# The norms behind two attentions in two parts, in a two-block transformer kernel on one Trainium2 core

## The reference

```python
# block 1: two attentions side by side, 8 heads of 64 each
oa = dsa_attention(...)          # (1, 512, 512)
ob = forgetting_attention(...)   # (1, 512, 512)
o = jnp.concatenate([rms_norm(oa, g_out_a), rms_norm(ob, g_out_b)], axis=-1)
x = x + gate_m * (o @ w_out)     # 1024 x 1024
h = rms_norm(x, g_ffn) * (1.0 + scale_f) + shift_f
g_logits = h @ w_group ...; e_all = h @ w_router ...        # 4 + 32 columns, then the experts

# block 2: differential attention, 8 heads of 128, 768 keys
o = diff_attention(q, k_all, v_all, lam)                    # (1, 512, 8, 128)
o = rmsnorm(o, subln_g) * (1.0 - lam_init)                  # per head
y_attn = o.reshape(B, L, ATTN_OUT) @ w_branch_attn          # 1024 x 1024
y = (g_attn * y_attn + g_sgu * y_sgu) @ w_out
```

## Time and profile before

| | µs |
|---|---|
| median of 3 runs | 2796.1 |
| lowest and highest | 2791.27, 2798.64 |
| the profiled execution, its own time | 2799.37 |
| its span | 2797.6 |
| PE busy in it | 2667.5 (95%) |
| mean granted PE clock, share of full | 0.973 |

### The profile page before, as it was taken

How to read it: one execution, slowest core, us unless ns; L and a number is a source line. 1 busy time by engine, 2 the same in 40 slices (tenths; PEclk the granted TensorE clock), 3 DMA queues, 4 the chain that set the end, 5 groups by cost and what they waited for, 6 DMA issues and landing times. The chain is left out here.

```text
span 2797.6 us, 37221 instructions
## 1 busy us (share of the span) xinstructions
PE 2667.5 (95%) x14205; PEld 2184.3 (78%) x14209; DVE 1795.8 (64%) x3171; ACT 1074.9 (38%) x1724; POOL 922.6 (33%) x468
## 2 busy tenths in 40 slices
PE   8998898889999999999899999999999999999999
PEld 5776784333477878878787899999999978888887
DVE  7959442111142537439754099998998967889888
ACT  3225733223243322137633233334555533333333
POOL 0011122222224430112141357886322224455542
PEclk9996999999999999999999999999999999999999
DMA  8830048999633345300322147886689799999995
GB/s 354 310 114 1 3 160 332 386 400 381 256 131 121 122 173 196 126 25 1 121 90 93 61 140 249 300 297 218 238 306 327 286 354 387 376 397 393 388 407 219
DMA packets 135471, 646.34 MB, mean 231 GB/s; under 512 B 21536, under 2 KB 22432, under 8 KB 91040
## 3 DMA queue, kind: packets, MB, share of 16 engines
q1 hardware_dynamic: 86224, 485.11, 46.1%
q0 software_dynamic: 48384, 158.38, 15.1%
q10 hardware_dynamic: 720, 0.96, 0.1%
HBM read 620.25 MB, written 75.50 MB: 249 GB/s over the span
## 5 line engine op out<-in xcount | busy, mean ns | idle before, releaser
L195 PE MATMUL psum<-h_hi,w_hi 128*128 128x384 f32 (+1 forms) x1808 | 664.0, 367 | 18.3 <-DVE h_lo L575 4.4
L197 PE MATMUL psum<-h_hi,w_lo 128*128 128x384 f32 (+1 forms) x1808 | 651.8, 361 | 0.0
L196 PE MATMUL psum<-h_lo,w_hi 128*128 128x384 f32 (+1 forms) x1808 | 651.8, 360 | 0.0
L176 POOL TENSOR_TENSOR w_lo<-ring,w_hi 128x2048 fp32r<-128x2048 f32 x45 | 210.5, 4678 | 730.0 <-ACT w_hi L169 547.5
L195 PEld LDWEIGHTS psum<-h_hi,w_hi 128*128 128x128 f32 x1808 | 341.9, 189 | 54.4 <-issue 24.0
L196 PEld LDWEIGHTS psum<-h_lo,w_hi 128*128 128x128 f32 x1808 | 341.9, 189 | 32.6 <-issue 1.9
L197 PEld LDWEIGHTS psum<-h_hi,w_lo 128*128 128x128 f32 x1808 | 341.2, 189 | 33.0
L2589 ACT ACTIVATE w_hi<-ring 128x2048 fp32r<-128x2048 f32 x127 | 242.5, 1909 | 215.8 <-PE psum L197 196.6
L195 PE MATMUL psum<-w_hi,a_hi 128*128 128x512 f32 x768 | 300.8, 392 | 5.6 <-DVE w_lo L2597 5.6
L196 PE MATMUL psum<-w_lo,a_hi 128*128 128x512 f32 x768 | 299.7, 390 | 0.0
L197 PE MATMUL psum<-w_hi,a_lo 128*128 128x512 f32 x768 | 299.6, 390 | 0.0
(11 more groups left out here) (494 smaller groups left out, 4637.7 us busy)
## 6 DMA issues: line engine op xcount, KB each, us to landing
ring<-in_weights SPq DMA_DIRECT2D x199, 1024.0 KB, 6.9
w_expert_in<-in_experts_in SPq DMA_DIRECT2D x32, 2048.0 KB, 12.2
hid_dram<-hid_acts SPq DMA_DIRECT2D x64, 384.0 KB, 5.2
gates_dram<-block_gates SPq DMA_DIRECT2D x24, 1024.0 KB, 11.3
hid_tiles<-hid_dram SPq DMA_DIRECT2D x62, 384.0 KB, 7.7
gate_tiles<-gates_dram SPq DMA_DIRECT2D x15, 1536.0 KB, 13.0
o<-in_ada_later SPq DMA_DIRECT2D x16, 1024.0 KB, 6.3
w_expert_down<-in_experts_down SPq DMA_DIRECT2D x16, 1024.0 KB, 12.0
```

Source lines behind the costliest of these rows:

```text
L176: eng.tensor_tensor(lo, slot(k, n), hi.bitcast(F32), ALU.subtract).then_inc(k.w_ready, 1)
L195: k.nc.tensor.matmul(out, hi, x_hi, start=start, stop=False)
L196: k.nc.tensor.matmul(out, hi, x_lo, start=False, stop=False)
L197: return k.nc.tensor.matmul(out, lo, x_hi, start=False, stop=stop)
```

## The change

Each norm is cut into an early part and a late part. The early part holds the groups of columns that the attention finishes first: columns 512 to 1023 at the first joint (4 chunks), heads 0 to 6 at the second (7 chunks). Its sums, root, inverse, scaling and turns now stand in the attention stage, ahead of the barrier: DVE and ACT do their share between the last units, PE turns behind its last weighing (`turn_early`). The late part stays in the second stage. The contraction order of `first_products` puts the early chunks first (`norm.order`), and PE turns the late pieces at step 2 (first joint) or step 5 (second). Before the first product PE gets 8 idle products (`keep_going`). ACT splits the next weight tile (`between`) ahead of the late chunks instead of behind all eight. The `before` load loses its wait (it now goes to columns 512 to 639 of row tile 3). The scratch for sums, gains and the idle cell lies in tiles that exist already.

```diff
-def first_products(k, pe, outs, tile, source, done, ready):
+def first_products(k, pe, outs, tile, source, done, norm, turn_late_at):
     wait_split(k, pe, tile)
     hi, lo = parts(k, tile)
-    for kc in range(KC):
-        ready(min(kc + 1, KC - 1))
+    for step, kc in enumerate(norm.order):
+        if step == turn_late_at:
+            norm.turn_late(pe)
+        norm.split(pe, max(step, 1))
...
 class HeadNorm:
...
+        self.early, self.late = early, range(early.stop, self.groups) if early.start == 0 else range(0, early.start)
+        self.order = [g * per_group + c for part in (self.early, self.late) for g in part for c in range(per_group)]
...
     def vector(self, dve):
...
+        self.sum_squares(self.late)
+        low(0)
+        low(1)
+        self.invert(dve, self.late, 1)
+        for t in self.by_vector(self.late_by_scalar):
+            self.scale_by_vector(t, self.late)
+        for step in range(2, KC):
+            low(step)
...
+    def scalar(self, act, between):
...
+        high(0)
+        high(1)
+        self.root(act, self.late, 1)
...
+        for t in self.late_by_scalar:
+            self.scale_by_scalar(t, self.late)
+        for step in range(2, self.n_early):
+            high(step)
+        between()
+        for step in range(self.n_early, KC):
+            high(step)
...
@@ attention_stage: early = group 1, ACT scales row tile 3 early and tiles 2, 3 late
+                norm.turn_early(pe)
...
+                    if t == n:
+                        dve.wait_ge(square_done, 2 * first_sparse)
+                        norm.sum_early(dve)
+                    if t == n + 1:
+                        norm.invert_early(dve)
+                        for i in norm.by_vector(norm.early_by_scalar):
+                            norm.scale_by_vector(i, norm.early)
...
+                    if t == n:
+                        norm.load_root()
+                        norm.root_early(act)
+                    if t == n + 1:
+                        square(t - DEEP - 3)
+                    if t == n + 3:
+                        norm.scale_early_by_scalar(act)
...
@@ out_projection_stage
-                norm.rows_read(sp)
                 sp.dma_start(before, k.d["before"]).then_inc(consts, 16)
...
-                norm.tensor(pe)
-                first_products(k, pe, [k.psum[:, c] for c in range(2)], first, (k.h_hi, k.h_lo), done, lambda kc: norm.split(pe, kc))
+                keep_going(k, 7, 8)
+                first_products(k, pe, [k.psum[:, c] for c in range(2)], first, (k.h_hi, k.h_lo), done, norm, 2)
...
@@ diff_attention_stage: early = heads 0 to 6, ACT scales row tile 3 early and none late
+                pe.wait_ge(out_copied, n - 1)
+                norm.turn_early(pe)
...
+                    if t == n + 1:
+                        dve.wait_ge(square_done, n - TT)
+                        norm.sum_early(dve)
+                        norm.invert_early(dve)
+                    if t > n:
+                        norm.scale_by_vector(t - n - 1, norm.early)
...
+                    if t == n + 3:
+                        norm.scale_early_by_scalar(act)
                     if t > DEEP + 1:
                         square(t - DEEP - 2)
+                    if t == n:
+                        norm.load_root()
+                        norm.root_early(act)
```

More of the change, by code:

```diff
@@ L659, in attention_stage @@
     DEEP = 3
+    norm = k.norm = HeadNorm(k, k.squares[:], k.head_total, k.vecs[:, G_OUT:G_OUT + KC], range(1, 2), ((3,), (2, 3)))
     def new_keys(q):
@@ new lines, in __init__, with part, rows, sum_squares @@
+        self.gains, self.idle = k.head_gains, k.head_idle
+    def part(self, view, groups):
+        return view[:, :, groups.start:groups.stop]
+    def rows(self, t, groups):
+        return self.k.o[:, t, groups.start * self.width:groups.stop * self.width].rearrange("p (g n) -> p g n", g=len(groups))
+    def sum_squares(self, groups):
+        nc, total = self.k.nc, self.part(self.total, groups)
+        if self.squares.shape[-1] > 1:
+            self.k.vstep(nc.vector.tensor_reduce(total, self.part(self.squares, groups), AX.X, ALU.add))
+        nc.vector.tensor_scalar(total, total, 1.0 / self.width, EPS, ALU.mult, ALU.add).then_inc(self.k.head_norm_sems[0], 1)
@@ new lines, in scale_by_scalar, with by_vector, sum_early @@
+    def scale_by_scalar(self, t, groups):
+        for g in groups:
+            part = self.k.o[:, t, g * self.width:(g + 1) * self.width]
+            ins = self.k.nc.scalar.activation(part, part, ACT.Copy, scale=self.total[:, t, g:g + 1])
+        ins.then_inc(self.k.head_norm_sems[2][self.turn], 1)
+    def by_vector(self, by_scalar):
+        return [t for t in range(TT) if t not in by_scalar]
+    def sum_early(self, dve):
+        self.sum_squares(self.early)
+        self.k.vstep(self.k.nc.vector.tensor_scalar(self.gains, self.gain, self.gain_scale, None, ALU.mult))
@@ new lines, in invert_early, with load_root, root, root_early @@
+    def invert_early(self, dve):
+        self.invert(dve, self.early, 0)
+    def load_root(self):
+        self.k.nc.scalar.activation(self.idle, self.k.eps[:, 0:1], ACT.Sqrt)
+    def root(self, act, groups, half):
+        std_ready, rooted = self.k.head_norm_sems[0], self.k.head_norm_sems[5]
+        total = self.part(self.total, groups)
+        act.wait_ge(std_ready, 4 * self.turn + 2 * half + 1)
+        self.k.nc.scalar.activation(total, total, ACT.Sqrt).then_inc(rooted, 1)
+    def root_early(self, act):
+        self.root(act, self.early, 0)
@@ new lines, in scale_early_by_scalar, with turn_rows @@
+    def scale_early_by_scalar(self, act):
+        act.wait_ge(self.k.head_norm_sems[0], 4 * self.turn + 2)
+        for t in self.early_by_scalar:
+            self.scale_by_scalar(t, self.early)
+    def turn_rows(self, pe, chunks, by_scalar, scaled_earlier):
+        k, nc = self.k, self.k.nc
+        _std_ready, scaled, scaled_by_scalar, turned, _copied, _rooted = k.head_norm_sems
+        by_vector = self.by_vector(by_scalar)
+        order = (*by_vector, *by_scalar)
+        for t in order:
+            if t in by_vector:
+                pe.wait_ge(scaled[self.turn], scaled_earlier[0] + by_vector.index(t) + 1)
+            else:
+                pe.wait_ge(scaled_by_scalar[self.turn], scaled_earlier[1] + by_scalar.index(t) + 1)
+            for c in chunks:
+                mm = nc.tensor.transpose(k.psum[:, self.order.index(c), t * P:(t + 1) * P], k.o[:, t, c * P:(c + 1) * P], k.ident[:])
+                if t == order[-1]:
+                    mm.then_inc(turned, 1)
@@ new lines, in scalar, with high @@
+    def scalar(self, act, between):
+        k, nc = self.k, self.k.nc
+        def high(step):
+            c = self.order[step]
+            act.wait_ge(k.head_norm_sems[3], KC * self.turn + step + 1)
+            nc.scalar.activation(self.parts[0][:, c], k.psum[:, step], ACT.Copy, scale=self.gains[:, c:c + 1]).then_inc(k.activation_high, 1)
+        high(0)
+        high(1)
+        self.root(act, self.late, 1)
+        if self.late_by_scalar:
+            act.wait_ge(k.head_norm_sems[0], 4 * self.turn + 4)
+        for t in self.late_by_scalar:
[5 more added lines that the diff above has]
+            high(step)
@@ L1050, in rows_read, with split @@
+    def split(self, pe, step):
+        pe.wait_ge(self.k.head_norm_sems[4], KC * self.turn + step + 1)
     def rows_read(self, eng):
@@ L2423, in stat @@
                 mm.then_inc(stat_done, 1)
[L2425 to L2426 removed]
+            keep_going(k, 7, 8)
+            first_products(k, pe, [k.psum[:, c] for c in range(2)], first, (branch_hi, branch_lo), branch_done.sem, norm, 5)
             for c in range(2, KC):
```

113 lines of the change are left out of this document (44 added, 69 removed).

## The result

| | median µs (lowest, highest) | ratio to the kernel before, 95% interval |
|---|---|---|
| before, measured beside it | 2798.59 (2790.61, 2805.11) | |
| the changed kernel | 2804.02 (2797.05, 2810.77) | 1.0022 (1.0014, 1.0030) |
| its profiled execution | 2805.09, span 2803.3 | |

One of the 20 executions of the changed kernel, a slow one of 10543.77 µs, is left out of its highest time and of the ratio. 1.0022 of 2797 is +6.2 µs, with an interval of +3.9 to +8.4 (the two medians of the table differ by 5.4); the forecast was +2.6. The whole interval lies above no change and within 0.3%. The page answers the earlier trace rows: PE's busy time grew by 9.6 µs and its count by 32 rows. These are the idle products, 8 at each joint; each makes two rows in the trace (x16), and the 8 take 2.02 µs in a wait. The other 5.6 µs of busy time are the same work; the mean granted clock fell from 0.973 to 0.971.

A forecast was written before the change was run, and what follows sets the result against it. PE, busy 95% of the span, was taken as the bound, with late loads holding both joints: first +0.3 + 0.9 = +1.2, second -0.4 + 1.8 = +1.4, sum +2.6 µs, giving 2798.7 against the median 2796.1; range 2791 to 2804.

The forecast's parts named there:

- Both norms leave the path, the barriers come 1.0 and 2.5 µs later.: Both joints: early norm work moves into the attention stage; the barriers come 1.0 µs later at the first, 2.5 at the second.
- The small load comes out behind the 6 MB wherever it is issued, and the first joint stays bound by it.: First joint: `before` lands behind the same 6 MB at 369.9, so PE's bias products start +0.3 µs later.
- x becomes the last of the three at the second joint.: Second joint: x lands at 1393.4, behind gates and u, and releases DVE's first gating step; -0.4 µs.
- The clock at the second joint, 1.8.: Second joint: PE's granted clock falls behind its 4.5 µs pause, costing 2.2 or 1.5 µs; 1.8 taken.
- The clock at the first joint, 0.9.: First joint: bias products and first logits run at a lowered clock behind PE's wait; bounds 0 and 2.2 µs, 0.9 taken.
- PE is the bound behind it and nothing gives the time back.: Behind the second joint: PE bounds the kernel, so that joint's loss of +1.4 µs is not recovered.
- the first (the clock costs nothing net): Both joints: loads bound, slow clock stretches replace the old ones one for one; +0.3 - 0.4, 2796.0 µs; chance 0.20.
- The second and third: First joint: small load lands early, 2791.8 µs, chance 0.08; both joints: PE's side decides, 2785.5 µs, chance 0.05.
- The fourth: Both joints: turns ahead of the barriers take 0.22 instead of 0.11 µs each; +5.9, 2802.0 µs; chance 0.15.
- The signs that the prediction listed: Both joints: `before` within 0.5 µs of w_expert_down, PE waits 5 to 6 and some 4, x releases gating, barriers later.

The follow-up runs named there:

- the second joint alone: Change made at the second joint only, the first joint's code as in the kernel before: median 2799.51 µs, ratio 1.0009 to the kernel before.
- the load edits: Changed kernel with the small load `before` issued first and x on its own semaphore: median 2784.74 µs, ratio 0.9958 to the kernel before.

## Why the prediction was wrong

Step by step, as it stood:

- **Both norms leave the path, the barriers come 1.0 and 2.5 µs later.** Right: 351.05 against 347.80 and 1377.89 against 1373.19, net 0.8 and 2.4, or 1.1 and 2.7 with the delay of the reference copies. The turns ran at 0.12 µs each.
- **The small load comes out behind the 6 MB wherever it is issued, and the first joint stays bound by it.** Right in mechanism, shown by moving it to the front: 17.1 µs became 1.7, and the share at the logits went from +3.2 to -7.4. The size was near: +0.3 forecast; +0.9 in the trace after, +0.1 to +0.4 in the five others with this joint and load, 0.3 more in each from the copies ahead.
- **x becomes the last of the three at the second joint.** Right, shown by waiting for it apart, and by the same edit doing nothing in the old kernel. -0.4 forecast, +0.6 measured (+0.2 to +0.6 over the traces), 0.3 more from the copies ahead: the barrier's share was right, but x took 18.0 µs instead of the 16.9 that I carried over from the earlier trace rows. This step failed by about 1 µs.
- **The clock at the second joint, 1.8.** Measured 1.9 at chunk 4 (1.9 to 2.1 in five traces, 2.8 in the one with the second joint alone).
- **The clock at the first joint, 0.9.** This term failed most within the joints. It was 2.3 up to the logits, 2.5 to 2.7 in the five other traces, above the upper bound of 2.2 that the text gave. I took less than half of the bound because the products behind the wait are small and "only partly array time". The trace says that they are wholly so: 16 of them took 3.60 µs at half clock and 1.87 at full, a factor of 1.93. And the old kernel's own slow microseconds, 373 to 376, did not stand in for the new ones: the slow stretch in the trace after reaches from the wait to 381.6. By the experts' first product 1.1 to 1.4 µs of this are given back in five of the six traces, so it is not the larger part of what is missing at the end.
- **"PE is the bound behind it and nothing gives the time back."** At the second joint nothing gave it back; but the sum ended there, and the loss did not. Another 1.6 µs went 100 µs further on, behind a pause of 2.1 µs that the old kernel has too. The prediction put this at nothing without looking there.

So of the 6.2 µs, 2.6 were forecast; the trace, up to the logits and the query keys, puts the difference at 0.6 and 1.0 for the two loads, 1.4 and 0.1 for the clock at the joints, and 1.6 for the clock further on, 4.7 in all (7.3 less 2.6), without the 0.3 at each joint. Of what lasts, most is missing at the second joint: +1.4 forecast, +3.7 to +4.5 measured, against +1.2 forecast and +1.4 to +2.9 measured for the first at the experts' first product. The direction and the two binding loads were right. What failed is the price of the clock at the first joint, the time that x takes to land, and above all a sum that ended at the second joint while the clock's loss went on.

Of the rivals, the first (the clock costs nothing net) falls by the idle products in the waits, which took the second share from +4.1 to +0.3 and about 0.9 off the first, with the loads landing as in the other traces. The second and third (early load, PE's side decides) describe what the load edits then brought about, not the change. The fourth named nearly the right time (2802.0) by a mechanism that wasn't there: the turns ran at full clock. The range reached to 2804.0 on its account and the median fell just above it. The signs that the prediction listed came true, two of them larger than said: the small load 0.2 µs behind the 6 MB, PE's wait for it (6.5 µs for 5 to 6), DVE released by x, PE waiting for POOL's tile (5.5 µs for 4), the two barriers. None of them would have shown the clock's true price.

**What stays open:** why the clock falls at the two pauses ahead of the query only behind the new joint; why u and x take 0.8 µs longer from issue to landing; and whether the longer idle products at the query are worth anything with both load edits.

## What to carry to other kernels

When work is moved ahead of a barrier, list every transfer that starts at the barrier and ask which of them is needed first: here 64 KB at the end of a queue of 6 MB, and a wait for three tensors where two were needed, cost the whole gain of nearly 12 µs, and two edits of a few lines gave it back (ratio 0.9958). Issue the small load that is needed first ahead of the large ones, and give each consumer a semaphore for just what it reads. Price a new wait on a matrix engine as its length plus the work behind it at half clock, in full, small products included, and look for pauses that were harmless before.

## What the runs showed of the hardware

- The clock's loss repeats by program. Falls of the granted clock behind the second joint were the same in two traces of each kernel and the same in kernels that share the code, and where some are removed another can come up: 0.66, 0.83, 0.83, 1.00 as changed, 0.66, 1.00, 1.00, 0.83 with more idle products at the query. Not every fall costs time: the one behind the pause of 2.1 µs took 1.6 µs, the one behind the pause of 2.6 nothing that shows.
- Products of 36 columns are slowed by the clock as much as wide ones: 3.60 against 1.87 µs for 16, where those of 512 columns start every 0.43 against 0.23 µs.
- Turns of 128x128 pieces against the identity kept the clock at full: 16 and 28 of them, 1.92 and 3.51 µs, at 1.00 behind the weighing. In the kernel before PE did nothing but turns from 351.0 to 356.9, and the clock came back to full among them (0.74 from 355 to 356).
- The same code is not the same length in each execution: the stage of the experts took between 305.7 and 314.2 µs over the traces, more than the whole effect under study; up to there the kernel with the second joint alone is the kernel before, and it took 306.4 against 314.2 and 310.8. A share read inside a trace repeated within 0.8 µs up to the logits and at the second joint; the length of a whole trace did not.
- The 64 KB load took 12.0 or 17.1 µs from issue to landing behind the same 6 MB, issued 9.1 and 4.7 µs behind the opening, and 1.7 when it stood first in SP's list.
